# x's convolution of a Mamba-2 layer: kept in rows with partition-shifted DMA copies, instead of transposed to columns and back

## The reference, cut to what matters

```python
xbc = jax.nn.silu(causal_depthwise_conv(xbc, conv_w, conv_b))      # 4 taps
xs, Bm, Cm = jnp.split(xbc, [SSM_D_INNER, SSM_D_INNER + G * N], axis=-1)
dt = softplus(dt_raw + dt_bias)
y = ssd_chunked(xs, dt, A, Bm, Cm)            # (C B^T * decay) @ (xs * dt)
y = y + d_skip[..., None] * xs
y = y * silu(z);  y = y * rsqrt(mean(y * y over a group) + eps) * norm_w
```

## Time and profile before

| | |
|---|---|
| median of 3 runs | 2050.89 us (2050.73 to 2051.79) |
| the profiled execution | 2051.72 us |
| its span, first to last instruction | 2050.1 us |
| TensorE busy | 2040.8 us (100% of the span) |
| VectorE, ScalarE, GpSimd busy | 1566.3, 1172.0, 171.6 us |
| DMA | 419.80 MB, mean 205 GB/s |
| one group of the changed stage | 50.75 us (704.79 to 755.54) |

### The profile page before, as it was taken

The page is one execution under the profiler, slowest core; times in us unless marked ns, Lnnn a source line. Parts: engine busy times, 40 slices in busy tenths (PEclk is TensorE's granted clock), DMA queues, the critical chain, the costliest instruction groups (busy, mean ns, idle before and its releaser), DMA issues.

```text
span 2050.1 us, 28075 instructions
## 1 busy us (share of the span) xinstructions
PE 2040.8 (100%) x9580; PEld 1677.7 (82%) x9580; DVE 1566.3 (76%) x1861; ACT 1172.0 (57%) x1496; POOL 171.6 (8%) x195
## 2 busy tenths in 40 slices
PE   9999999999999999999999999999999999999999
PEld 8888877778888888888888888888888888887887
DVE  6777866665856777777667887888898889877866
ACT  5444655555556666666655554556666666645543
POOL 1121000000011222222000000010000000000000
PEclk9999999999999999999999999999999999999999
DMA  7656675654566666666565657598888888667574
GB/s 250 199 182 203 188 220 166 176 162 152 182 204 186 185 185 184 185 190 187 167 192 183 212 168 238 177 307 244 258 254 237 250 259 250 196 205 232 176 246 154
DMA packets 220626, 419.80 MB, mean 205 GB/s; under 512 B 16449, under 2 KB 22002, under 8 KB 220290
## 3 DMA queue, kind: packets, MB, share of 16 engines
q1 hardware_dynamic: 212162, 399.48, 61.8%
q0 software_dynamic: 7776, 18.94, 4.4%
q10 hardware_dynamic: 608, 0.34, 0.1%
HBM read 410.25 MB, written 4.26 MB: 202 GB/s over the span
## 4 chain that ended last, share of the span: by engine, by line
PE 92%; DVE 3%; DMA 2%; ACT 1%; issue 0%; SPq 0%; DVEq 0%; ACTq 0%
PE acc L2246 72%; PE side L2333 8%; PE acc L2333 6%; PE side L2262 3%; DMA w_raw<-in_w_ffn_down 1%; DVE w_lo L2038 1%; PE side L2402 1%; PE side L2549 1%; DVE w_raw L1953 0%; ACT w_hi L1216 0%; DVE w_lo L1257 0%; DMA x_row<-in_x 0%; DMA w_raw<-in_w_in 0%; PE acc L2262 0%; ACT w_hi L724 0%
## 5 line engine op out<-in xcount | busy, mean ns | idle before, releaser
L1257 DVE TENSOR_TENSOR w_lo<-w_raw,w_hi 128x1024 fp32r<-128x1024 f32 x332 | 420.7, 1280 | 245.7 <-ACT w_hi L724 244.5
L724 ACT ACTIVATE w_hi<-w_raw 128x1024 fp32r<-128x1024 f32 x332 | 348.5, 1057 | 355.7 <-PE acc L2246 315.2
L2246 PE MATMUL acc<-w_hi,h_hi 128*128 128x512 f32 x1248 | 498.7, 400 | 0.2
L2246 PE MATMUL acc<-w_hi,h_lo 128*128 128x512 f32 x1248 | 487.0, 390 | 0.0
L2246 PE MATMUL acc<-w_lo,h_hi 128*128 128x512 f32 x1248 | 485.9, 389 | 0.0
L2246 PEld LDWEIGHTS acc<-w_hi,h_hi 128*128 128x128 f32 x1248 | 234.4, 188 | 52.7 <-issue 7.0
L2246 PEld LDWEIGHTS acc<-w_hi,h_lo 128*128 128x128 f32 x1248 | 234.3, 188 | 50.3
L2246 PEld LDWEIGHTS acc<-w_lo,h_hi 128*128 128x128 f32 x1248 | 234.7, 188 | 47.6 <-issue 1.9
L1932 DVE TENSOR_TENSOR w_lo<-w_raw,w_hi 128x1024 fp32r<-128x1024 f32 x136 | 165.1, 1220 | 38.0 <-ACT w_hi L1137 35.4
L1053 ACT ACTIVATE w_hi<-w_raw 128x1024 fp32r<-128x1024 f32 x110 | 116.6, 1061 | 117.2 <-PE acc L2246 70.2
L1137 ACT ACTIVATE w_hi<-w_raw 128x1024 fp32r<-128x1024 f32 x136 | 142.9, 1057 | 65.8 <-PE acc L2246 50.4
(11 more groups left out here) (436 smaller groups left out, 3445.9 us busy)
## 6 DMA issues: line engine op xcount, KB each, us to landing
w_raw<-in_w_in SPq DMA_DIRECT2D x320, 512.0 KB, 4.3
w_raw<-in_w_ffn_down SPq DMA_DIRECT2D x88, 512.0 KB, 4.9
w_raw<-in_w_ffn_gate SPq DMA_DIRECT2D x68, 512.0 KB, 4.6
w_raw<-in_w_ffn_up SPq DMA_DIRECT2D x68, 512.0 KB, 5.2
w_raw<-in_w_ssm_proj SPq DMA_DIRECT2D x64, 512.0 KB, 4.4
side_raw<-in_w_ffn_up SPq DMA_DIRECT2D x40, 512.0 KB, 4.7
w_raw<-in_w_attn_proj SPq DMA_DIRECT2D x32, 512.0 KB, 3.7
w_raw<-in_w_out SPq DMA_DIRECT2D x32, 512.0 KB, 4.7
```

The lines of the kernel that those rows point to most:

```text
L724: nc.scalar.activation(w_hi[:, r], w_raw[:, n % RING], ACT.Copy).then_inc(hi_ready, 1)
L1257: nc.vector.tensor_tensor(w_lo[:, r], w_raw[:, n % RING], w_hi[:, r].bitcast(F32), ALU.subtract).then_inc(lo_ready, 1)
L2246: done = nc.tensor.matmul(acc[p][:, t], a[:, k0 + kk, cut], w[:, r, kk], start=first and kk == n == 0, stop=last and kk == UK - 1 and n == ...
```

## The change

The convolution stays in rows. A shift in time is then a shift over partitions, and DMA makes it: `earlier[back - 1]` is x_proj moved down by `back` partitions, for back = 1, 2, 3. For each of the three the sync engine issues one copy of partitions 16 to 127; ScalarE issues one copy of partitions `back` to 15 and one of the last `back` rows of the first half of time, which become the first rows of the second half. GpSimd loads the taps and the bias of the group, broadcast over the partitions (4 x 512 and 512 elements). VectorE multiplies the four tiles by their taps and adds three times and once the bias, ScalarE makes the SiLU in place in x_proj; VectorE, and GpSimd for d_skip, then read x_proj. Both sets of 8 transposes, and the copy to y_row, are gone.

Steps that move: `y_products` from x1 to x4, `y_rows` from x3 to x6, `y_columns` from z0 to z3 (TensorE); `tail_gated` from x3 to x6, `tail_transposed` from z1 to z4, `decays` to z6 and z7, xdt and xdt_end to x0 of the next group (VectorE); `exps` to z4 and z5, the `y_cols` copy to x4, `tail_squares` to z0, and `tail_normed`, now ScalarE's, to z2. GpSimd: d_skip now comes before the masks of the next group, and the loads of the taps behind them. Each x chunk on TensorE can start as soon as ScalarE has copied the one before.

```diff
@@ buffers
-        conv_x = at("conv_x", 191, [P, CT, T])
+        earlier = [at(f"earlier{n + 1}", kb, [P, TT, CW]) for n, kb in enumerate((138, 142, 175))]
+        taps_b = at("taps_b", 167, [P, TAPS, CW])
+        conv_bias_b = at("conv_bias_b", 191, [P, 1, CW])
@@ sync engine
-                chunk(w_in, (i + i) * (CW // 2) + COL_Z)
+                for u in range(UPC):
+                    if u == UPC - 1:
+                        sp.wait_ge(x_rows_ready, i + 1)
+                        for back in range(1, TAPS):
+                            sp.dma_start(earlier[back - 1][16:P], x_proj[16 - back:P - back]).then_inc(shift_in, 16)
+                    load(w_in, u * UK, (i + i) * (CW // 2) + COL_Z)
@@ ScalarE
+            def conv_silu(g):
+                act.wait_ge(conv_ready, g + 1)
+                nc.scalar.activation(x_proj[:], x_proj[:], ACT.Silu).then_inc(xs_ready, 1)
+            def tail_normed(g):
+                act.wait_ge(y_rstd, g + 1)
+                for t in range(TT):
+                    last = nc.scalar.activation(y_row[:, t], y_row[:, t], ACT.Copy, scale=y_scale[:, t:t + 1])
+                last.then_inc(y_ready, 1)
@@ ScalarE, end of x_chunk
+                if not head:
+                    act.wait_ge(xdt_ready, g)
+                    act.wait_ge(skip_ready, g)
                 for t in range(TT):
                     last = nc.scalar.activation(x_proj[:, t], acc[0][:, t], ACT.Copy, scale=x_rstd[:, t:t + 1])
                 last.then_inc(x_rows_ready, 1)
+                act.wait_ge(x_rows_ready, g + 1)
+                nc.scalar.sem_inc(acc_free[0], 1)
+                for back in range(1, TAPS):
+                    nc.scalar.dma_start(earlier[back - 1][back:16], x_proj[0:16 - back]).then_inc(shift_in, 16)
+                    nc.scalar.dma_start(earlier[back - 1][0:back, 1], x_proj[P - back:P, 0]).then_inc(shift_in, 16)
@@ ScalarE, z_chunk
-                    if u == 0:
-                        act.wait_ge(x_T, g + 1)
-                        for n in range(CT):
-                            last = conv_first_taps(sums(0)[:, n], g * CT, conv_x[:, n], n)
-                        last.then_inc(conv_first, 1)
...
-                    if u == 5:
-                        act.wait_ge(xdt_ready, g + 1)
-                        nc.scalar.activation(y_row[:], side[:, 2:4], ACT.Copy).then_inc(xrow_ready, 1)
+                    if u == 0 and not head:
+                        tail_squares(g - 1)
+                    if u == 2 and not head:
+                        tail_normed(g - 1)
+                    if u in (4, 5):
+                        exps(g, u - 4, head)
+                    if u == 6:
+                        conv_silu(g)
@@ VectorE
+            def by_taps(tile, back):
+                return nc.vector.tensor_tensor(tile[:], tile[:], taps_b[:, TAPS - 1 - back].unsqueeze(1).broadcast_to([P, TT, CW]), ALU.mult)
+            def conv_step(g, u):
+                if u == 2:
+                    dve.wait_ge(shift_in, g * 144 + 144)
+                    dve.wait_ge(taps_in, g * 32 + 32)
+                    by_taps(earlier[0], 1)
+                    by_taps(earlier[1], 2)
+                if u == 3:
+                    by_taps(earlier[2], 3)
+                    by_taps(x_proj, 0).then_inc(taps_read, 1)
+                if u == 4:
+                    dve.wait_ge(taps_read, g + 1)
+                    nc.vector.tensor_tensor(earlier[0][:], earlier[0][:], earlier[1][:], ALU.add)
+                    link(nc.vector.tensor_tensor(x_proj[:], x_proj[:], earlier[2][:], ALU.add))
+                if u == 5:
+                    link(nc.vector.tensor_tensor(x_proj[:], x_proj[:], earlier[0][:], ALU.add))
+                    nc.vector.tensor_tensor(x_proj[:], x_proj[:], conv_bias_b[:].broadcast_to([P, TT, CW]), ALU.add).then_inc(conv_ready, 1)
@@ VectorE, z_chunk: after split_lo() of step u
+                    if u == 4 and not head:
                         tail_transposed(g - 1)
+                    conv_step(g, u)
+                    if u in (6, 7):
+                        decays(g, u - 6)
@@ GpSimd
+            def taps_load(g):
+                ours = conv_w[0][:, bass.ds(g * CW, CW)]
+                pool.dma_start(taps_b[:], ours.partition_broadcast(P)).then_inc(taps_in, 16)
+                pool.dma_start(conv_bias_b[:], conv_b[:, bass.ds(g * CW, CW)].partition_broadcast(P)).then_inc(taps_in, 16)
+            def next_group(i, first=False):
                 pool.wait_ge(decay_exp, i * 2 + 2)
                 loads(i + 1)
+                skip(i, first)
+                masks(i + 1)
+                pool.wait_ge(y_sum, i + 1)
+                taps_load(i + 1)
                 tail(i)
@@ TensorE, z_between
                     if u == 0:
-                        pe.wait_ge(x_rows_ready, g + 1)
-                        for n in range(CT):
-                            for t in range(TT):
-                                at_col = (n % 2) * T + t * P
-                                last = transpose(acc[0][:, n // 2, at_col:at_col + P], x_proj[:, t, n * P:(n + 1) * P])
-                        last.then_inc(x_T, 1)
...
+                    if u == 3 and not first:
+                        y_columns(g - 1)
+                    if u == 6 and not first:
+                        pe.wait_ge(yT_ready, g)
-                    if u == 4:
...
-                        for n in range(CT):
-                            for t in range(TT):
-                                last = transpose(side[:, 2 + t, n * P:(n + 1) * P], conv_x[:, n, t * P:(t + 1) * P])
-                        last.then_inc(xs_T, 1)
```

More of the change, by code:

```diff
@@ L1602, in _ @@
                 nc.vector.tensor_tensor(gated, acc[c % 2][:], gated, ALU.mult).then_inc(acc_free[c % 2], 1)
+            for back in range(1, TAPS):
+                last = nc.vector.memset(earlier[back - 1][0:back, 0], 0.0)
+            link(last)
             def tail_gated(g):
@@ L1632, in tail_transposed @@
                                         ALU.mult).then_inc(yT_ready, 1)
-            def x_chunk(g, head):
-                for u in range(UPC):
-                    split_lo()
-                    if not head:
-                        if u == 3:
-                            tail_gated(g - 1)
-                        if u == 6:
-                            tail_normed(g - 1)
-            def conv_taps(g, back):
-                for n in range(CT):
-                    last = conv_other_taps(sums(0)[:, n], g * CT, conv_x[:, n], n, back)
-                if back < TAPS - 1:
-                    link(last)
-                else:
-                    last.then_inc(conv_done, 1)
             def decays(g, hf):
@@ new lines, in x_scaled @@
+            def x_scaled(g):
+                by_head = "p (h d) -> p h d"
+                dve.wait_ge(xs_ready, g + 1)
+                for t in range(TT):
+                    last = nc.vector.tensor_tensor(
+                        xdt[:, t].rearrange(by_head, d=HP), x_proj[:, t].rearrange(by_head, d=HP),
+                        dt[:, t, bass.ds(g * HG, HG)].unsqueeze(2).broadcast_to([P, HG, HP]), ALU.mult)
+                last.then_inc(xdt_ready, 1)
+                dve.wait_ge(xdt_ready, g + 1)
+                nc.vector.tensor_tensor(
+                    xdt_end[:].rearrange(by_head, d=HP), xdt[:, 0].rearrange(by_head, d=HP),
+                    edge[:, 0, bass.ds(g * HG, HG)].unsqueeze(2).broadcast_to([P, HG, HP]), ALU.mult).then_inc(xdt_end_ready, 1)
@@ L1662, in z_chunk, with tail_step, x_chunk @@
+            def tail_step(g, u):
+                if u == 0:
+                    x_scaled(g)
+                if u == 6:
+                    tail_gated(g)
+            def x_chunk(g, head):
                 for u in range(UPC):
                     split_lo()
-                    if u == 0:
-                        dve.wait_ge(conv_first, g + 1)
-                        for back in range(1, TAPS):
-                            conv_taps(g, back)
-                    if u == 1 and not head:
-                        tail_transposed(g - 1)
@@ L1670, in z_chunk @@
[L1670 to L1692 removed]
+                    if not head:
+                        tail_step(g - 1, u)
@@ L1694, in _, with z_chunk @@
+            def z_chunk(g, head):
+                for u in range(UPC):
+                    split_lo()
+                    if u == 4 and not head:
+                        tail_transposed(g - 1)
+                    conv_step(g, u)
+                    if u in (6, 7):
+                        decays(g, u - 6)
             x_chunk(0, True)
+            dve.wait_ge(edge_ready, 1)
             z_chunk(0, True)
```

97 lines of the change are left out of this document (31 added, 66 removed).

## The result

The changed kernel takes **2098.94 us** (median of 4 runs, 2097.51 to 2103.1) against 2051.34 for the kernel before beside it: ratio 1.0233, 95% interval 1.0215 to 1.0251, slower by 47.6 us. The forecast was 2050, its range ended at 2066.

What follows compares the result with a forecast made beforehand. TensorE, busy for all of the span, was taken as the bound. Saved transposes, -13.4 us, and collisions with GpSimd, +12.3, sum to -1.1 us: 2049.8, say 2050, on the median of 2050.89; 8-in-10 range 2038 to 2066.

Steps and rivals of the forecast that it cites:

- TensorE, -13.4: On TensorE, dropping both sets of eight transposes saves 1.67 us a group, 13.4 us over 8 groups.
- GpSimd and VectorE, +12.3: Masks and d_skip collide with VectorE's instructions, making x0's split 1.0 and xdt 0.75 us late: 1.75 a group, 12.3 us.
- xdt blocked as I took it: At x0, xdt now reads SBUF and is held by GpSimd's second mask; if not, 2044.5 us.
- The first half of that rule: On VectorE, an instruction with at most one SBUF input stays clear of GpSimd.
- the collisions eat the gain: Likeliest case: VectorE's collisions with GpSimd cancel the transposes' saving, 2045 to 2056 us; chance 0.45.
- ScalarE's issues: Six issues before z0's split take 2.9 us, hidden; rival: slower issues delay y_columns, 2053.5 to 2060 us, chance 0.12.
- The value of 0.49 and the bound of 0.63: Price in us of one DMA issue by ScalarE: 0.49 expected, 0.63 as high bound.
- The copies and z7's weights: SP's copies land by about 9.5 us, z7's load by 11.5: nothing taken, bounds 0 and 3 us a group.
- z7's weights behind the copies: Rival: z7's load, queued behind taps, z6's load and copies, lands too late for VectorE's chain: 2064 us, chance 0.15.
- VectorE's margin of 3.3 us: Without GpSimd, x0's split would be done near 31.0 us, while TensorE asks for it at 34.3.
- its own last sign: Forecast is wrong if TensorE waits anywhere else than named, or by more than 3 us a group.
- Both slower ones: Two slower rivals: z7's weights landing late behind the copies, chance 0.15, and dearer issues by ScalarE, chance 0.12.

Runs made afterwards that it cites:

- run 3: Changed kernel without all nine copies (shifted tiles zero), GpSimd's two masks and the bias of the decays' exponentials: 2035.67 us, ratio 0.9922 to the kernel before.
- run 2: Changed kernel with all nine copies of each group and the wait for them left out, shifted tiles zero: 2051.6 us, ratio 0.9998 to the kernel before.
- run 4: Changed kernel without SP's three large copies, ScalarE's six small ones kept: 2070.47 us, ratio 1.0093 to the kernel before.
- run 7: Changed kernel without the loads of the taps and of all groups' bias but the first, multiplying by the bias tile instead: 2083.51 us, ratio 1.0149.
- run 1: Changed kernel with SP issuing z7's weights ahead of the three large copies: 2114.29 us, ratio 1.0312 to the kernel before.
- run 5: Changed kernel without ScalarE's six small copies, SP's three large ones kept: 2093.61 us, ratio 1.0206 to the kernel before.
- run 6: Changed kernel with the six small copies issued by GpSimd instead of ScalarE: 2098.57 us, ratio 1.023 to the kernel before.
- run 18: Changed kernel with the six small copies issued by GpSimd and GpSimd's masks moved behind its tail: 2072.51 us, ratio 1.0104 to the kernel before.
- run 8: Changed kernel with the same bytes in six copies instead of nine, SP's three taking rows from `back` on: 2253.76 us, ratio 1.0983.
- run 12: Changed kernel with y_columns and y^T one unit later and GpSimd's masks behind its tail: 2139.32 us, ratio 1.0428 to the kernel before.

## Why the prediction was wrong

Point by point, in its order:

- **TensorE, -13.4.** Right, a little small: 15.7 us once nothing stands in the way (run 3).
- **GpSimd and VectorE, +12.3.** Right in mechanism and place. In run 2 the last split and xdt take 3.43 and 3.47 us, xdt blocked as I took it. TensorE waited up to 1.0 us for the split as forecast, and 0.4 instead of 0.75 for xdt; the price of the masks as a whole was 15.9 (run 2 less run 3). The Trainium skill's rule in "SBUF — State Buffer", Who interferes with whom, said that xdt, with two SBUF inputs in its new place, would be held; the trace agrees, 3.47 us for what took 1.28. The first half of that rule, as the prediction gives it, lacks the section's exception for VectorE's 2-port modes; the scaling of y_row in the earlier trace rows, with one tensor in SBUF, was held too: 3.02 us for the two, 2.62 of them for the first, where the median of one is 0.48. The likeliest case, "the collisions eat the gain", is what the kernel without its copies does: 2051.6 against 2049.8.
- **ScalarE's issues: the first step that failed.** The value of 0.49 and the bound of 0.63 came from issues of other copies at other places; these six take 0.64 to 1.33, 0.92 on average in the group shown, more in others. z0's split starts at 851.0. Counted from z0's start (856.85 less the wait of 2.35 less 11.6 = 842.9) that is 8.1, and 6.3 was forecast. y_columns is 2.35 late: the rival "ScalarE's issues" as it was written, at a price beyond its upper end. By itself it costs 19 us (run 4), where the rival's upper end was 10; beside the large copies, but without the taps, the run is 32 us over the one without copies, and y_row is the only large wait (run 7).
- **The copies and z7's weights: the second, and alone the larger.** "I take nothing, bounds 0 and 3 us a group". Two terms were off. The rate: 303 GB/s was extrapolated from a share of 0.61; at 0.98 the engines moved 248. And what else is in flight: the copies were to land by 9.5 and VectorE had them at 17.3 (860.17), because the taps' 1.3 MB are in flight with them (run 7), and 512 KB more ahead of them cost another 15 us (run 1). The rival "z7's weights behind the copies" had the bytes. It put the landing at 12.9 (a slip: 12.3 us from -0.6 on end at 11.7, which by its own limit of 12.6 costs nothing) where ScalarE had the weights at 18.4 (861.25), and looked at the weights, while the copies themselves came last for VectorE. Alone they cost 42 us (run 5).
- **VectorE's margin of 3.3 us** held only with the multiplications at 11.3, behind a split at 10.2. They start at 17.3, 6 us later, so y^T is 2.2 us late. The forecast had no term for y^T at all; by its own last sign (a wait anywhere else, or over 3 us a group) it was wrong.
- **The clock was not in the sum.** Behind waits as those of 2.20 and 4.3 us TensorE ran at 1.2 GHz for a time, which in the kernel before it never did in this stretch (1.00). That is 17.4 us against run 2, two thirds as much as the idle time (26.0 us more than in run 2).
- **The rivals were taken one at a time.** Both slower ones happened together, with chances of 0.12 and 0.15. Since each hides part of the other, neither cure alone shows (run 6 gave nothing; 18 gave 26 us with the masks moved).

Settled: the copies carry all of the loss. Without the taps' bytes beside them 15 us of it go and 32 stay; alone the small ones cost 19 and the large ones 42. The collisions with the masks cost 16, which is all that the transposes give. Not tried: loading the taps earlier, since their tile lies under the decays' tile; issuing all nine copies from GpSimd, and moving the masks behind the tail with nothing else changed. So how the 26 us of run 18 divide between masks and issues stays open.

## What to carry to other kernels

An engine that is busy all the time gains from removed work only if what replaces it arrives in time: price a new transfer by the bytes already queued ahead of it and at the rate of full DMA engines, and price an issue by the same kind of copy from the same engine. Look at how many instructions on an in-order engine stand between a late arrival and the next thing that TensorE asks for; moving a consumer one step later helps nothing if it passes more of them. When two delays cover each other, undoing one shows no gain: take both away before a theory is dropped.

## What the runs showed of the hardware

- With a copy of 127 partitions in flight the DMA engines moved 23 GB/s (run 8); with copies of 112 partitions, and the other rows in small ones, 248 GB/s at a share of 0.98. The runs move the same bytes and are 155 us apart.
- An issue of a copy inside SBUF took ScalarE 0.73 to 0.84 us (medians, without SP's copies beside it), GpSimd 0.51, SP 0.59 without the taps' loads and 0.98 with them.
- The same matmuls took 17.4 us more behind waits of 2 to 4 us, against 26.0 us more of idle time; of two neighbouring groups with such waits one had a granted clock of 0.97 and one of 1.00.
- Two masks moved onto two splits took 5.72 us and the splits 6.56, and TensorE hardly waited for a split (0.4 us in all, run 18); ahead of a late y^T the masks' move cost 18 us (run 12).
